# Expert weights loaded by groups of 1024 columns, and down rows four to a partition

## What is computed

```
logits = h @ w_router                      # h: 256 tokens x 1024
top_v, top_i = top_k(logits, 2)            # of 8 experts
gates = softmax over the two, 0 elsewhere
a = h @ w_gate[e];  u = h @ w_up[e]        # w_gate, w_up: 8 x 1024 x 3584
act = silu(a) * u * gates[:, e]
y = sum over e of act @ w_down[e]          # w_down: 8 x 3584 x 1024
```

## Time and profile before

| | |
|---|---|
| median of 3 runs | 2480.89 us |
| span of the profiled execution | 2484.7 us |
| mean granted TensorE clock | 0.973 |
| PE, PEld busy | 2373.0, 1776.1 us |
| DVE, ACT busy | 642.0, 372.1 us |
| HBM read over the span | 579.58 MB |
| expert stage on PE (first L2281 to last L2328) | 696 to 1605 us |

### The profile page before, as it was taken

The page is one execution under the profiler, slowest core; times in us unless marked ns, Lnnn a source line. Parts: engine busy times, 40 slices in busy tenths (PEclk is TensorE's granted clock), DMA queues, the critical chain, the costliest instruction groups (busy, mean ns, idle before and its releaser), DMA issues.

```text
span 2484.7 us, 38130 instructions
## 1 busy us (share of the span) xinstructions
PE 2373.0 (96%) x16705; PEld 1776.1 (71%) x16706; DVE 642.0 (26%) x1802; ACT 372.1 (15%) x931; POOL 28.0 (1%) x52
## 2 busy tenths in 40 slices
PE   7999999998999999999998999799899999989999
PEld 4768888877866568855654565486588888658888
DVE  3663634148310000000000000134531112552111
ACT  3222000123210000000000000124410002431001
POOL 1010000001000000000000000000000000000000
PEclk8998999998899999999999999999899999989999
DMA  9373586623179999899999999953234442324410
GB/s 357 129 271 124 211 322 224 213 94 136 68 281 349 386 394 392 288 375 394 394 394 395 390 392 390 350 177 138 102 136 157 148 135 79 135 76 144 161 68 17
DMA packets 270072, 583.09 MB, mean 235 GB/s; under 512 B 19386, under 2 KB 46530, under 8 KB 269908
## 3 DMA queue, kind: packets, MB, share of 16 engines
q1 hardware_dynamic: 268900, 579.51, 63.9%
q10 hardware_dynamic: 432, 1.01, 0.1%
q0 software_dynamic: 576, 0.13, 0.0%
HBM read 579.58 MB, written 1.05 MB: 234 GB/s over the span
## 4 chain that ended last, share of the span: by engine, by line
PE 85%; DMA 5%; DVE 4%; SPq 2%; ACT 2%; issue 1%; DVEq 0%; ACTq 0%
PE acc L1595 12%; PE wrk L2281 11%; PE acc L848 9%; PE wrk L3006 9%; PE wrk L1578 6%; PE acc L2328 5%; PE wrk L2265 4%; PE acc L851 4%; PE wrk L2288 3%; DMA ring<-in_moe_w_gate_dram 2%; DMA ring<-in_moe_w_down_dram 2%; PE acc L922 2%; PE acc L2316 2%; PE acc L937 2%; PE acc L2334 2%; SPq L482 1%
## 5 line engine op out<-in xcount | busy, mean ns | idle before, releaser
L2281 PE MATMUL wrk<-ring,hT 128*64 128x256 f32 x3136 | 356.9, 383 | 20.4 <-DMA ring<-in_moe_w_up_dram 9.9
L2281 PEld LDWEIGHTS wrk<-ring,hT 128*64 128x64 f32 x3136 | 221.8, 137 | 138.6 <-issue 24.8
L1595 PE MATMUL acc<-scratch,ring 128*128 128x256 f32 x1376 | 300.3, 379 | 0.0
L1595 PEld LDWEIGHTS acc<-scratch,ring 128*128 128x128 f32 x1376 | 261.2, 190 | 35.4
L848 PE MATMUL acc<-hT,ring 128*128 128x256 f32 (+2 forms) x1152 | 263.5, 385 | 1.3 <-ACT scratch L878 0.5
L848 PEld LDWEIGHTS acc<-hT,ring 128*128 128x128 f32 (+2 forms) x1152 | 211.3, 186 | 42.8 <-issue 4.4
L3006 PE MATMUL wrk<-hT,ring 128*128 128x256 f32 x1024 | 223.3, 379 | 0.0
L3006 PEld LDWEIGHTS wrk<-hT,ring 128*128 128x128 f32 x1024 | 194.6, 190 | 26.5
L2528 DVE TENSOR_TENSOR scratch<-scratch,wrk 128x256 f32<-128x256 f32 (+1 forms) x49 | 23.5, 479 | 687.3 <-PE wrk L2281 344.9
L2328 PE MATMUL acc<-ring,scratch 128*64 128x512 f32 x784 | 180.2, 602 | 17.2 <-DMA ring<-in_moe_w_down_dram 15.2
L1578 PE MATMUL wrk<-hT,ring 128*128 128x256 f32 x704 | 154.8, 380 | 0.0
(11 more groups left out here) (410 smaller groups left out, 2098.1 us busy)
## 6 DMA issues: line engine op xcount, KB each, us to landing
ring<-in_moe_w_gate_dram SPq DMA_DIRECT2D x56, 2048.0 KB, 19.3
ring<-in_moe_w_up_dram SPq DMA_DIRECT2D x56, 2048.0 KB, 20.8
ring<-in_moe_w_down_dram SPq DMA_DIRECT2D x56, 2048.0 KB, 19.1
ring<-in_w_ada_dram SPq DMA_DIRECT2D x24, 2048.0 KB, 15.0
ring<-in_w_up_dram SPq DMA_DIRECT2D x16, 2048.0 KB, 8.6
ring<-in_w_down_dram SPq DMA_DIRECT2D x16, 2048.0 KB, 8.0
ring<-in_w_out_dram SPq DMA_DIRECT2D x8, 2048.0 KB, 8.8
ring<-in_w_in_dram SPq DMA_DIRECT2D x8, 1536.0 KB, 12.6
```

The lines of the kernel that those rows point to most:

```text
L1595: mm = pe.matmul(accv[:, m, :], w[:, j, m * P:(m + 1) * P], F_ACT[:, 4 * (g % 2) + j, :], start=(g == 0 and j == 0 and m % 2 == 0), stop=( ...
L2281: mm = pe.matmul(wrk[half * HD:half * HD + HD, bank, 0:S], hT[:, k, 0:HD], w[:, k, half * S:half * S + S], start=(k == 0), stop=(k == KD - ...
```

## The change

Gate and up weights of an expert are taken in groups of 1024, 1024, 1024 and 512 columns. A group of 1024 has two items for each of gate, up and down. A gate or up item of such a group holds four of the eight row blocks (k) and all 1024 columns, so it lies in HBM in runs of 1024 floats, 4 KB. A down item still holds 512 rows, but in the three wide groups partition p has rows 4p to 4p+3, one run of 16 KB. The last group, of 512, has items as before. The number and the size of the items stay: 21 of 2 MB an expert, through the same seven slots.

So that the activations meet the rows of their partition, the other operand is picked with a step of four floats (16 bytes) in the wide groups: the heavy expert's stationary weights (`tile_columns`), the moving weights of the 32-token part of a middle expert (`part` in `quarters`), and the activations that `turn_light` transposes (`turn_columns`). The 64-token halves stream neighbouring columns, now 512 of them a matmul.

One group's gate product now fills two PSUM banks and its up product the other two, with no second set. ACT and DVE work once on a whole group, in heavy experts too. The gather of the next expert stands before the last `down_`. Heavy experts' down loop (`fall`) walks the two items of the group and reads `H_ACT` in neighbouring columns. The general path for many tokens (`experts_any_*`) is rewritten in the same way and not run with these inputs. The core of the diff:

```diff
+EXPERT_GROUPS = [(f, min(1024, F_EXPERT - f)) for f in range(0, F_EXPERT, 1024)]
+
+
+def expert_items(kind, g):
+
+    return [(kind, g, b) for b in range(EXPERT_GROUPS[g][1] // 512)]
...
-    n = len(ffn_groups(F_EXPERT))
+    n = len(EXPERT_GROUPS)
     for g in range(n):
-        experts += [("egate", g), ("eup", g)]
+        experts += expert_items("egate", g) + expert_items("eup", g)
         if g:
-            experts.append(("edown", g - 1))
-    experts.append(("edown", n - 1))
+            experts += expert_items("edown", g - 1)
+    experts += expert_items("edown", n - 1)
...
                 def expert_load(item, n, which):
-                    f, w = groups[item[1]]
-                    src = sources[item[0]][0][which]
-                    if item[0] == "edown":
-                        sp.dma_start(ring[:, n % SLOTS, 0:w * KD].rearrange("p (j d) -> p j d", d=D),
-                                     src[f:f + w].rearrange("(j p) d -> p j d", p=P)).then_inc(landed[n % SLOTS], 16)
+                    kind, g_, b = item
+                    f, w = EXPERT_GROUPS[g_]
+                    src = sources[kind][0][which]
+                    if kind == "edown":
+                        f += 512 * b
+                        order = "(p j) d -> p j d" if w == 1024 else "(j p) d -> p j d"
+                        sp.dma_start(ring[:, n % SLOTS, :].rearrange("p (j d) -> p j d", d=D),
+                                     src[f:f + 512].rearrange(order, p=P)).then_inc(landed[n % SLOTS], 16)
                     else:
-                        sp.dma_start(ring[:, n % SLOTS, 0:w * KD].rearrange("p (k f) -> p k f", k=KD),
-                                     by_rows(src)[:, :, f:f + w]).then_inc(landed[n % SLOTS], 16)
+                        ks = SLOT // w
+                        sp.dma_start(ring[:, n % SLOTS, :].rearrange("p (k f) -> p k f", k=ks),
+                                     by_rows(src)[:, ks * b:ks * b + ks, f:f + w]).then_inc(landed[n % SLOTS], 16)
...
+        M_SIL, M_ACT, M_TURNED = Z(0, 768), Z(768, 768), Z(1536, 2, 768)
+        L_SIL, L_ACT, L_TURNED = Z(9786, 512), Z(10298, 512), Z(10810, 2, 512)
+        H_ACT, H_SIL = Z(0, 2, D), Z(2048, D)
+        E_ACT = [Z(0, 8, S), Z(9786, 8, S)]
+        GATE_AT, UP_AT = 0, 1024
+        flat_wrk = wrk[:, :, :].rearrange("p b n -> p (b n)")
...
+        def expert_cols(item):
+
+            w = EXPERT_GROUPS[item[1]][1]
+            return slot_of(item).rearrange("p (k f) -> p k f", k=SLOT // w)
+
+        def expert_rows(item):
+            return slot_of(item).rearrange("p (j d) -> p j d", d=D)
+
+        def item_ks(item):
+
+            n = SLOT // EXPERT_GROUPS[item[1]][1]
+            return [(n * item[2] + i, i) for i in range(n)]
+
+        def last_item(kind, g):
+            return expert_items(kind, g)[-1]
+
+        def tile_columns(g, j):
+
+            if tiles_of(g) == 4:
+                return slice(j * P, (j + 1) * P)
+            return slice(512 * (j // 4) + j % 4, 512 * (j // 4) + 512, 4)
+
+        def turn_columns(g, c):
+
+            per_half = tiles_of(g) // 2
+            if per_half == 2 or c >= per_half:
+                return slice(c * P, (c + 1) * P)
+            return slice(c, 512, 4)
...
+            def banks_read(e, g, kind):
+
+                if kind == "egate":
+                    pe.wait_ge(ffn_silu, tile_of(e, first_tile(g)))
+                else:
+                    pe.wait_ge(ffn_act, tile_of(e, first_tile(g)))
+                    turned_before = thin_slice(e, g if thin(e) else 0)
+                    if turned_before:
+                        pe.wait_ge(light_ready, turned_before)
+
             def rise(e, g):
+                for kind, lo in (("egate", GATE_AT), ("eup", UP_AT)):
+                    banks_read(e, g, kind)
+                    for item in expert_items(kind, g):
+                        arrive(e, item)
+                        w = expert_cols(item)
+                        for j in range(tiles_of(g)):
+                            for k, at_ in item_ks(item):
+                                mm = pe.matmul(flat_wrk[:, lo + j * P:lo + (j + 1) * P], w[:, at_, tile_columns(g, j)], hT[:, k, 0:P],
+                                               start=(k == 0 and j % 4 == 0), stop=(k == KD - 1), skip_group_check=True)
+                        mm.then_inc(freed_by_pe, 1)
+
+            def rise_light(e, g):
+                n2, n4 = half_width(g), quarter_width(g)
+                for kind, lo in (("egate", GATE_AT), ("eup", UP_AT)):
+                    banks_read(e, g, kind)
+                    for item in expert_items(kind, g):
+                        arrive(e, item)
+                        w = expert_cols(item)
+
+                        def halves():
+                            for k, at_ in item_ks(item):
+                                for h in range(2):
+                                    mm = pe.matmul(flat_wrk[h * HD:h * HD + HD, lo:lo + n2], hT[:, k, 0:HD], w[:, at_, h * n2:(h + 1) * n2],
+                                                   start=(k == 0), stop=(k == KD - 1), skip_group_check=True)
+                            return mm
+
+                        def quarters():
+                            for k, at_ in item_ks(item):
+                                for c in range(4):
+                                    if n2 == 512:
+                                        part = w[:, at_, (c // 2) * 512:(c // 2) * 512 + 512].rearrange("p (x j) -> p j x", j=4)
+                                        part = part[:, 2 * (c % 2):2 * (c % 2) + 2, :]
+                                    else:
+                                        part = w[:, at_, c * n4:(c + 1) * n4].rearrange("p (j x) -> p j x", j=1)
+                                    mm = pe.matmul(flat_wrk[quarter(c), lo + n2:lo + n2 + n4].rearrange("p (j x) -> p j x", x=P),
+                                                   hT[:, k, LIGHT:MIDDLE], part, start=(k == 0 and n2 == 512), stop=(k == KD - 1),
+                                                   skip_group_check=True)
+                            return mm
+
+                        if not middle(e):
+                            mm = halves()
+                        elif item[2] == 0:
+                            halves()
+                            mm = quarters()
+                        else:
+                            quarters()
+                            mm = halves()
+                        mm.then_inc(freed_by_pe, 1)
+
+            def turn_light(e, g):
+                pe.wait_ge(ffn_act, tile_of(e, first_tile(g) + tiles_of(g)))
+                held = M_ACT if middle(e) else L_ACT
+                for c in range(thin_width(e, g) // P):
+                    mm = pe.transpose(flat_wrk[:, UP_AT + c * P:UP_AT + (c + 1) * P], held[:, turn_columns(g, c)], ident)
+                mm.then_inc(light_turned, 1)
+
...
+            def fall_light(e, g):
+                pe.wait_ge(light_ready, thin_slice(e, g) + 1)
+                turned = (M_TURNED if middle(e) else L_TURNED)[:, g % 2, :]
+                per_half, per_quarter = half_width(g) // P, quarter_width(g) // P
+                for item in expert_items("edown", g):
                     arrive(e, item)
...
                 up_(e, 2)
-                down_(e, 1)
-                if thin(e):
-                    turn_light(e, 2)
                 if e:
                     pe.wait_ge(share_added, 2 * e)
                 pe.wait_ge(picked, 4 * e + 2)
                     for t in range(2):
                         mm = pe.transpose(acc[:, 2, S + t * P:S + (t + 1) * P], m_wpick[:, t, P:S], ident)
                 mm.then_inc(pick_turned, 1)
+                down_(e, 1)
+                if thin(e):
+                    turn_light(e, 2)
                 up_(e, 3)
                 down_(e, 2)
                 if thin(e):
                 if e + 1 < NE:
                     pe.wait_ge(pick_ready, e + 1)
                     gather(e + 1)
-                for g in range(4, E_LAST + 1):
-                    up_(e, g)
-                    down_(e, g - 1)
-                    if thin(e):
-                        turn_light(e, g)
-                down_(e, E_LAST)
+                down_(e, 3)
...
+            def gates(e, g, place, width):
+                act.wait_ge(*expert_freed(e, "egate", g))
+                act.wait_ge(ffn_act, tile_of(e, first_tile(g)))
+                act.activation(place[:, 0:width], flat_wrk[:, GATE_AT:GATE_AT + width], ACT.Silu).then_inc(ffn_silu, tiles_of(g))
```

More of the change, by code:

```diff
@@ L303, in program @@
         free, counts = {}, {"pe": 0, "dve": 0, "up": 0}
-        UP_TILES = sum(n // P for _, n in ffn_groups(F_EXPERT))
-        FREED = sum(1 for i in EXPERTS if i[0] != "eup")
+        UP_TILES = F_EXPERT // P
+        FREED = len(EXPERTS)
         def note(n, item):
@@ L311, in note @@
                 free[n] = (freed_by_dve, counts["dve"], 0)
-            elif kind in ("up", "eup", "mup"):
```

(60 more changed lines are left out.)

225 lines of the change are left out of this document (80 added, 145 removed).

## The result

The changed kernel takes 2602.21 us (median of four runs, 2594.14 to 2604.99) against 2481.39 us: a ratio of 1.048, 95% interval 1.046 to 1.050, slower. The forecast was 2589, in a range of 2450 to 2645.

What follows compares the result with a forecast made beforehand. PE's own work (874 of the 909 us stage) and transfers lay close together. PE became 874 + 82 + 57 + 5 - 1 = 1017 us with all waits gone: stage +108, 2593 less 3.8 gives 2589 us, range 2450 to 2645.

Steps and rivals of the forecast that it cites:

- the 35 us of waits go, all of them: Expert stage: slower PE work leaves the ring full after a heavy expert, so all 35 us of PE's waits vanish.
- 232 us of PE for a pair with 213 of transfer: A light plus a middle expert: 86 + 146 us of PE against 213 of transfer, so PE bounds.
- That part alone would be -27 us: Weight transfers: longer runs save 25 us after 1080 us and 2 us of waits in expert 1.
- the same: Middle experts' 32-token part, unstepped: 256 neighbouring columns take 1.93 us an item against 1.95 with 128.
- no change: Light halves: an item as 32 records of 256 columns takes 3.67 us, as sixteen of 512 columns 3.65.
- 1.72 ns a column: PE's 16-byte stepped loads and streams: price taken from L1401, the only stepped row, against 0.9 for neighbouring columns.
- the bound of 91 us: Heavy expert's stepped gate and up loads: upper cost if L1401's 0.116 us a load holds; +82 was taken.
- `turn_light` had +5: 84 stepped transposes in seven experts: each 0.22 us load hides half behind its predecessor, +5 us (0 to 9).
- The order of the work had -1: Single PSUM bank set, first transpose of expert 0 and earlier gather: together -1 us.
- rival 1: PE's stepped operands: 16-byte steps are free, so transfers decide; 2454 us, between 2445 and 2465, chance 0.20.
- Rival 3: Middle experts' 32-token part: four streams share a partition's reads; 2646 us, or over 2900 fully in line; chance 0.05.
- the +27 us for that: Heavy expert: half of its other 55 us of work at the lower clock level would add 27 us.

Runs made afterwards that it cites:

- experiment 2: The changed kernel with its 16 KB down runs kept, but PE's operands taken as neighbouring columns (output not the reference's): 2448.38 us, 0.987 of before.
- long_runs_no_step: Kernel name of experiment 2: the changed kernel with 16 KB down runs but no stepped operands; 2448.38 us, 0.987 of before.
- step_of_two: The changed kernel with two 8 KB runs a partition in wide down items and all three operands stepped by 8 bytes: 2458.34 us, 0.990 of before.

## Why the prediction was right, and where it was off

**What bounds.** Right. Two bounds lay close together, PE's own work and the stream, and the change moved the first past the second. The signs that were named came: records of the heavy line (194.2 - 14.5)/768 = 0.234 us apart, transfers at 332 GB/s over the stage, and more than 410 GB/s where only wide down items move (433 in experiment 2). A step that failed, in a small way, is "the 35 us of waits go, all of them": 7.0 stayed. A timeline of PE in expert 3, right behind the heavy one, shows where (start us, us, then what):

```profile
1238.27 3.65 PE L2408 MATMUL acc<-ring,scratch 128*64 128x512 f32 x16 [1.05 <-DMA ring<-in_moe_w_down_dram]
1243.16 3.65 PE L2408 MATMUL acc<-ring,scratch 128*64 128x512 f32 x16 [1.24 <-DMA ring<-in_moe_w_down_dram]
```

The forecast compared 232 us of PE for a pair with 213 of transfer, and that average hides the light half: its 21 items at 405 GB/s are 109 us of transfer, 5.2 us each, and PE eats them in 86. At its start (1168.5) six items lie in the ring and the next is just issued; 70 us bring 13 more, and PE is then at its 19th, so even this ring is empty for the last down items.

**Transfers.** "That part alone would be -27 us" was right: 17.6 us are the gate and up runs and 8.0 the down runs, 25.6 in all. The stage itself fell by 24.5 us with 4 KB runs and by 32.5 with the 16 KB ones, 6.9 more than the transfers give, and this is a term put at zero. The forecast had the 32-token part at "the same", 1.93 for 1.95 us an item; that line took 77.6 us instead of 82.1 without steps. The halves, "no change" in the forecast, went from 356.9 to 347.5 us after the change, the light down line from 180.2 to 177.1. Together, the stage without its waits for weights is 876.2 - 20.6 = 855.6 us in long_runs_no_step against 873.9 before: 18.3 us of PE's own work that the forecast kept.

**Steps.** Right in mechanism, low in size. The forecast of 1.72 ns a column, taken from L1401, was 1.83. The 1.72 had the run-out of the last record taken off; the 0.116 us as they stand in the row are 1.81 ns and gave the bound of 91 us. The loads cost 93 us instead of 82, the streams 68 instead of 57 against the same matmuls without the step. `turn_light` had +5 and got 0.6 us of stage (1.8 of PE's busy time), within its bounds of 0 to 9. The order of the work had -1; only the waits for ACT at the down line show it (2.0 us before, none at that line after).

**The sum.** Stage +108 forecast, +114.6 measured: PE's own work +143 against +142.4 (1016.3 - 873.9), waits for weights -35 against -27.8. That the first pair agrees so closely is luck. The steps alone cost 93.3 + 68.0 + 1.8 = 163 us of PE where 144 were forecast, 19 too few, and the rest of PE's work fell by 18 us where 1 was forecast; the two errors cancel. By experts the forecast said about 240 us for the heavy one and 146 for a middle one, and 248.0 and 144.9 are in the windows; the 256-column matmuls that were to take over 500 ns take 631. The other half of the 13 us by which 2589 was low is outside the stage. The forecast took 3.8 us off the profiled span to reach the median, as before's was; the profiled execution of after is the fastest of its four, its span 10.1 us below the median, while its stage began 5.4 us earlier than before's and the rest behind the stage was 1.8 us shorter.

**The rivals.** Free steps of 16 bytes were rival 1. Its time of 2454 lies between the two kernels without steps (2456 with 4 KB runs, 2448 with the 16 KB ones), so what it said of the transfers holds, and only its price of a step was wrong. Rival 3, four streams that share what a partition can read, fails: a set of four takes 133.4/1148 x 4 = 0.465 us for 256 columns, 1.82 ns a column, what one load pays. Nor did the clock fall: the heavy expert's window shows 1.00, so the +27 us for that did not come.

The page "SBUF — State Buffer" of the Trainium skill, section "Door 1: The DMA port swizzle", has memory lines of 16 bytes and wants two hits in each. The runs bear this out for loads and streams: two hits at 8 bytes are nearly free, one hit at 16 bytes doubles the price. The same paragraph goes on that one can stride for free up to "4 fp32"; a step of four float32 is exactly the one that costs 1.83 instead of 0.88 ns here, so the measurement decides against that reading.

## What to carry to other kernels

Before data is laid out for longer transfers, price the step at which TensorE then reads it: with float32, 16 bytes cost twice as much for each stepped load and stream, 8 bytes next to nothing (one-record loads of transposes excepted, see below). Look in which part of the stage the slower work falls: where the ring is full it is paid in full, where the transfers bind a share comes back as shorter waits (13 of 68 us here). Longer runs pay in a stage bound by transfers (2 to 4 KB: 17.6 us of 909), and they can be had without a step by taking more columns of the same rows.

## What the runs showed of the hardware

- The rate of the weight stream by its runs in the loaded stretch: 387 to 391 GB/s with gate and up at 2 KB, 400 at 4 KB, 405 with six down items an expert at 16 KB. With one kind alone on the way it is 386 at 2 KB, 410 at 4 KB and 433 at 16 KB. Items of 1 MB instead of 2 MB make no difference (884.2 us of stage both times).
- A piece of one line's matmuls has 0.1 to 0.2 us to itself: 64 records take 3.66 us in one piece and 2 x 1.93 in two, less their overlap.
- Four streams of 256 columns side by side, out of the same partitions with a 16-byte step, take 1.82 ns a column, as long as a single load.
- The transposes don't fit the price by lines. Their load, 141 ns by the median with neighbours, takes 209 ns with 16 bytes and already 205 with 8 bytes (step_of_two), where the heavy expert's loads take 192, 329 and 196. Why the 8-byte step is slow there and not in the two-record loads was not tried.
